# A two-block transformer kernel on one core: one opening stage, modulation parts in the key preparation, an unrolled first attention, and three weight buffers with indexed stores in the second experts

## What is computed

```python
# first block; x (1024, 1024), ctx (256, 1024)
mod_lat = silu(c) @ w_ada + b_ada            # w_ada (1024, 6144): six parts of 1024
mod_ctx = silu(c_ctx) @ w_ada + b_ada
sh1, sc1, gt1, sh2, sc2, gt2 = split(mod_lat, 6)
h_lat = rms_norm(x, norm_mix_g) * (1 + sc1) + sh1
h_ctx = rms_norm(ctx, norm_mix_g) * (1 + csc1) + csh1
proj = concat(h_ctx, h_lat) @ w_in
# differential attention, 4 heads, two score maps of width 64 per head, 1280 keys
a = softmax(s[0]) - lam * softmax(s[1]);  out = a @ v
# ... gated linear attention, out projection, then
x = x + gt1 * y;  h2 = rms_norm(x, norm_ffn_g) * (1 + sc2) + sh2
x = x + gt2 * moe(h2)                         # 32 experts, top 2
# second block: recurrent branch, causal attention, and at its end
h = h + moe_2(rmsnorm(h, norm2_g))            # 64 experts of hidden width 256, top 2
```

## Time and profile before

| | |
|---|---|
| median of 3 runs | 3930.11 us (3925.04 to 3935.51) |
| profiled execution | 3926.85 us, its span 3925.1 us |
| PE busy | 3098.5 us (79%) |
| DVE busy | 1792.8 us (46%) |
| ACT busy | 1248.2 us (32%) |
| POOL busy | 242.1 us (6%) |
| moved by DMA | 712.57 MB, mean 182 GB/s |

### The profile page before, as it was taken

How to read it: one execution, slowest core, us unless ns; L and a number is a source line. 1 busy time by engine, 2 the same in 40 slices (tenths; PEclk the granted TensorE clock), 3 DMA queues, 4 the chain that set the end, 5 groups by cost and what they waited for, 6 DMA issues and landing times. The chain is left out here.

```text
span 3925.1 us, 41291 instructions
## 1 busy us (share of the span) xinstructions
PE 3098.5 (79%) x14820; PEld 2213.1 (56%) x14820; DVE 1792.8 (46%) x2609; ACT 1248.2 (32%) x1544; POOL 242.1 (6%) x348
## 2 busy tenths in 40 slices
PE   6599966775657799999369789868999896777772
PEld 2488864453546688888257688744565783222220
DVE  0611126665655798888466411235655434111112
ACT  0301103444321577777345411223333310000001
POOL 0000021000000100000100000013000100000001
PEclk8699958997878799999679899989799996888886
DMA  6322117002043799999431132220001446999995
GB/s 284 114 74 91 60 48 284 0 0 72 28 158 123 297 408 406 405 406 401 175 95 38 31 96 81 82 74 10 1 1 38 155 149 237 417 421 422 421 422 237
DMA packets 192239, 712.57 MB, mean 182 GB/s; under 512 B 26564, under 2 KB 62071, under 8 KB 140664
## 3 DMA queue, kind: packets, MB, share of 16 engines
q1 hardware_dynamic: 144024, 575.25, 38.3%
q10 hardware_dynamic: 29664, 68.60, 4.5%
q0 software_dynamic: 18432, 67.12, 4.4%
HBM read 593.04 MB, written 117.87 MB: 181 GB/s over the span
## 5 line engine op out<-in xcount | busy, mean ns | idle before, releaser
L316 DVE TENSOR_TENSOR exp_w_low<-exp_raw,exp_w_high 128x2048 fp32r<-128x2048 f32 x192 | 437.1, 2290 | 70.7 <-ACT exp_w_high L2147 70.7
L2147 ACT CAST exp_w_high<-exp_raw 128x2048 fp32r<-128x2048 f32 x192 | 366.8, 1912 | 135.1 <-PE exp_ps_y L2119 58.3
L2355 PE MATMUL exp_ps_g<-exp_gu,exp_xT 128*64 128x512 f32 x1024 | 270.7, 689 | 125.2 <-DMA exp_gu<-in_exp_w 122.9
L2355 PEld LDWEIGHTS exp_ps_g<-exp_gu,exp_xT 128*64 128x64 f32 x1024 | 82.7, 158 | 292.8 <-issue 223.6
L2093 PE MATMUL exp_ps_g<-exp_w_low,exp_xT_high 128*128 128x512 f32 x512 | 206.5, 403 | 5.7 <-DVE exp_xT_low L316 5.7
L2094 PE MATMUL exp_ps_g<-exp_w_high,exp_xT_low 128*128 128x512 f32 x512 | 203.5, 397 | 0.0
L2095 PE MATMUL exp_ps_g<-exp_w_high,exp_xT_high 128*128 128x512 f32 x512 | 203.4, 397 | 0.0
L325 PE MATMUL inproj_ps<-inproj_w_high,h1T_high 128*128 128x512 f32 (+1 forms) x528 | 203.3, 385 | 0.0
L324 PE MATMUL inproj_ps<-inproj_w_high,h1T_low 128*128 128x512 f32 (+1 forms) x528 | 203.2, 385 | 0.0
L323 PE MATMUL inproj_ps<-inproj_w_low,h1T_high 128*128 128x512 f32 (+1 forms) x528 | 203.1, 385 | 0.0
L2464 DVE TENSOR_TENSOR exp_h<-exp_sg,exp_ps_g 128x256 f32<-128x256 f32 x32 | 19.5, 611 | 384.3 <-ACT exp_sg L2411 384.3
(11 more groups left out here) (546 smaller groups left out, 6853.1 us busy)
## 6 DMA issues: line engine op xcount, KB each, us to landing
exp_gu<-in_exp_w SPq DMA_DIRECT2D x64, 2048.0 KB, 17.6
exp_raw<-in_expert_w_gate SPq DMA_DIRECT2D x64, 1024.0 KB, 7.0
exp_raw<-in_expert_w_up SPq DMA_DIRECT2D x64, 1024.0 KB, 7.3
exp_raw<-in_expert_w_down SPq DMA_DIRECT2D x64, 1024.0 KB, 7.9
exp_dn<-in_exp_w SPq DMA_DIRECT2D x32, 2048.0 KB, 12.5
scratch_y<-exp_y ACTq DMA_DIRECT2D x64, 512.0 KB, 8.2
ada_slab<-in_w_ada SPq DMA_DIRECT2D x16, 1536.0 KB, 14.7
scratch_y<-da_zero SPq DMA_DIRECT2D x1, 15872.0 KB, 61.2
```

What stands on the lines that cost most here:

```text
L316: return nc.vector.tensor_tensor(low, x, high.bitcast(F32), ALU.subtract)
L2147: nc.scalar.copy(w_h[:, c], raw[:, b]).then_inc(w_high, 1)
L2355: last = nc.tensor.matmul(ps_g[side(e)], xT[:, par, k, side(e)], gu[:, par, :, e, k, :], start=(k == 0), stop=(k == KD - 1))
```

## The change

1. The constants, both tables, the first two modulation parts and the first normalisation become one block, `opening`. Only 2048 of the 6144 columns of `w_ada` are read there, in eight slabs that all have their own place, and all ten row tiles too. Four lanes are multiplied together. ACT squares the tiles, with the copies of the sums after the fifth. An `end_stage` follows.
2. Parts 2, 5, 3 and 4 are made in `diff_prepare`: 16 slabs of 1 MB in four buffers, a step of products behind each tile's turn, the bias as a product with a row of ones. The tiles of queries and keys get four buffers.
3. The first attention is written out over its 32 units without a loop. The turn of the weights runs two units behind the scores, the product with the values three; there are three buffers of weights. The queries are read where they are, without POOL's copy.
4. The second experts get a third pair of weight buffers. Slots without a token carry an index outside the tensors, and such rows are left out of the gather and of the store, which POOL now does by index. All of `y2` is filled with zeros in the first attention, not its overflow rows alone. `route` names the rows for both expert stages with four vector operations more.

```diff
+def opening(core, inp, tables, tiles, hT):
...
+                load_rows(0)
+                for k in range(KD):
+                    sp.dma_start(slab[:, k], w[:, k, 0:RUN]).then_inc(w_loaded[k], 16)
+                for i, (rows, _, _) in enumerate(tiles):
+                    sp.dma_start(xt[:, i], rows).then_inc(x_loaded[i], 16)
+                load_rows(1)
...
+                pe.wait_ge(made, 4)
+                turn_rows_of(0)
+                pe.wait_ge(c_ready, 2)
+                for k0 in range(0, KD, LANES):
+                    for k in range(k0, k0 + LANES):
+                        pe.wait_ge(w_loaded[k], 16)
+                    for b in range(BANKS):
+                        for k in range(k0, k0 + LANES):
+                            lane = slice(k % LANES * LANE, (k % LANES + 1) * LANE)
+                            last = nc.tensor.matmul(ps[lane, b], cs[:, k], slab[:, k, b * BANK:(b + 1) * BANK],
+                                                    start=(k0 == 0), stop=(k0 == KD - LANES))
+                last.then_inc(streamed, 1)
...
+                for i in range(n):
+                    pe.wait_ge(xn_ready, i + 1)
+                    if i >= 2:
+                        pe.wait_ge(half_a, i - 1)
+                        pe.wait_ge(half_v, i - 1)
+                    for k in range(KD):
+                        last = nc.tensor.transpose(ps[:, i % 2 * 2 + k // 4, k % 4 * P:(k % 4 + 1) * P],
+                                                   xt[:, i, k * P:(k + 1) * P], core.ident[:])
+                    last.then_inc(turned, 1)
+                turn_rows_of(1)
...
+                    square(i)
+                    if i >= 1:
+                        root(i - 1)
+                    if i == EARLY:
+                        act.wait_ge(streamed, 1)
+                        for b in range(0, BANKS, 2):
+                            nc.scalar.copy(sums[:, b * BANK:(b + 1) * BANK], ps[:, b]).then_inc(sums_copied[0], 1)
+                root(n - 1)
...
+                def low(i):
+                    dve.wait_ge(high_done, i + 1)
+                    low_part(nc, hT[1][:, :, i * P:(i + 1) * P], ht[:, i % 2], hT[0][:, :, i * P:(i + 1) * P]) \
+                        .then_inc(low_done, 1)
+
+                for i in range(n):
+                    dve.wait_ge(turned, i + 1)
+                    if i >= 2:
+                        dve.wait_ge(low_done, i - 1)
+                    for k in range(KD // 2, KD):
+                        last = evacuate(op, i, k)
+                    last.then_inc(half_v, 1)
+                    if i >= 1:
+                        low(i - 1)
+                low(n - 1)
...
-        norm_transpose(core, "norm1", tiles, hT)
+        opening(core, inp, tables, tiles, hT)
+        core.end_stage()
...
-        U = 2 * DA_H
+        U = TT * DA_H
         GROUPS = [range(c, min(c + 4, KT)) for c in range(0, KT, 4)]
         G = len(GROUPS)
-        COPIER = [1 if gi == 1 else 0 for gi in range(G)]
-        PER = [COPIER.count(0), COPIER.count(1)]
+        assert G == 3
+        TURN_LAG, WEIGH_LAG = 2, 3
...
+                    for n in range(U + WEIGH_LAG):
+                        if n < U:
+                            scores(n)
+                        turning, weighing = 0 <= n - TURN_LAG < U, 0 <= n - WEIGH_LAG < U
+                        if turning:
+                            turn_group(n - TURN_LAG, 0)
+                        if weighing:
+                            weigh_group(n - WEIGH_LAG, 0)
+                            weigh_group(n - WEIGH_LAG, 1)
+                        if turning:
+                            turn_group(n - TURN_LAG, 1)
+                        if weighing:
+                            weigh_group(n - WEIGH_LAG, 2)
+                        if turning:
+                            turn_group(n - TURN_LAG, 2)
...
+                    for n in range(U + TURN_LAG):
+                        turning = 0 <= n - TURN_LAG
+                        if turning:
+                            copy_turned(act, nc.scalar.copy, 0, n - TURN_LAG, 0)
+                        if n < U:
+                            t, h = n // DA_H, n % DA_H
+                            if n >= TURN_LAG + 1:
+                                act.wait_ge(a_turned, (n - TURN_LAG) * G)
+                            for m in range(2):
+                                act.wait_ge(nb_ready, 2 * n + m + 1)
+                                sums = l0[:, t % 2, h:h + 1] if m == 0 else st[:, n % 2, 5:6]
+                                nc.scalar.activation(p[:, n % (TURN_LAG + 1), m], ps[m][:, 0:NK], ACT.Exp,
+                                                     bias=st[:, n % 2, 2 + m:3 + m], scale=SCALE,
+                                                     accum_out=sums).then_inc(e_done, 1)
+                        if turning:
+                            copy_turned(act, nc.scalar.copy, 0, n - TURN_LAG, 2)
...
+                    for n in range(U + WEIGH_LAG):
+                        if n < U:
+                            for m in range(2):
+                                maximum(n, m)
+                        if 0 <= n - TURN_LAG < U:
+                            copy_turned(dve, V.tensor_copy, 1, n - TURN_LAG, 1)
+                        if n >= WEIGH_LAG and (n - WEIGH_LAG) % DA_H == DA_H - 1:
+                            read_results((n - WEIGH_LAG) // DA_H)
+                        if 0 <= n - 1 < U:
+                            difference(n - 1)
+                    dve.wait_ge(o_read, TT)
...
+    ORDER = (2, 5, 3, 4)
+    CHUNKS = len(ORDER)
+    PAIRS = KD // 2
+    STEPS = CHUNKS * PAIRS
+    WB = 4
...
+                for i in range(XB):
+                    load_x(i)
+                for j, m in enumerate(ORDER):
+                    sp.dma_start(bias[:, j], b_ada[:, m]).then_inc(bias_loaded, 16)
+                for i in range(WB):
+                    load_slabs(i)
+                for i in range(XB, STEPS):
+                    if i < KT:
+                        load_x(i)
+                    load_slabs(i)
+                sp.dma_start(gain[:], inp["norm_ffn_g"][0].partition_broadcast(P)).then_inc(gain_loaded, 16)
                 sp.dma_start(v[:], proj[:, 2 * W:3 * W].rearrange("(t p) n -> p t n", p=P)).then_inc(v_in, 16)
...
+                pe.wait_ge(bias_loaded, 16 * CHUNKS)
+                for i in range(STEPS):
+                    if i < KT:
+                        turn(i)
+                    conditions(i)
+                    j = i // PAIRS
+                    if j >= 1 and i % PAIRS < 2:
+                        wide_row(j - 1, i % PAIRS)
+                for h in range(2):
+                    wide_row(CHUNKS - 1, h)
...
-                ch.mark(V.tensor_copy(rt.row_tok[:], ps_t[:, 0:NB]))
+                ch.mark(V.tensor_scalar(absent[:], ps_t[:, 0:NB], 0.0, NOWHERE, ALU.is_equal, ALU.mult))
+                ch.link(V.tensor_scalar(tokf[:], ps_t[:, 0:NB], -1.0, 0.0, ALU.add, ALU.max))
+                ch.mark(V.tensor_copy(rt.row_tok[:], tokf[:]))
+                ch.mark(V.tensor_tensor(rt.row_from[:], tokf[:], absent[:], ALU.add))
+                ch.mark(V.tensor_tensor(rt.row_to[:], own_row[:], absent[:], ALU.add))
...
+    BUFS = 3
...
+            self.load_down(sp, b, b)
+
+    def clear_tokens(self, nc):
+        for b in range(2):
+            nc.gpsimd.memset(self.x[b][:], 0.0).then_inc(self.x_cleared, 1)
...
-                    sp.wait_ge(gu_done, n + 1)
-                    weights.load_gate_up(sp, n, par)
-                    sp.wait_ge(y_done, n + 1)
-                    weights.load_down(sp, n, par)
-
-                with sp.Fori(0, E // 2 - 1) as it:
-                    for par in range(2):
-                        load(it + 1, par)
+                def load(n, buf):
+                    sp.wait_ge(gu_done, n)
+                    weights.load_gate_up(sp, n, buf)
+                    sp.wait_ge(y_done, n)
+                    weights.load_down(sp, n, buf)
+
+                BUFS = weights.BUFS
+                rounds = E // BUFS - 1
+                with sp.Fori(0, rounds) as it:
+                    for b in range(BUFS):
+                        load(it * BUFS + (BUFS + b), b)
+                for n in range(BUFS * (rounds + 1), E):
+                    load(n, n % BUFS)
...
+                                            bounds_check=T - 1, oob_is_err=False) \
                         .then_inc(x_loaded[par], 16)
 
+                def scatter(half, par):
+                    n = half * 2 + par
+                    for z in range(2):
+                        pool.wait_ge(y_copied[z], n + 2)
+                    nc.gpsimd.tensor_copy(rows_to[par][:], rt.row_to[:, bass.ds(n, 1)]).then_inc(places_named, 1)
+                    pool.wait_ge(places_named, n + 1)
+
+                    pool.sem_inc(rows_seen, 1)
+                    pool.indirect_dma_start(out=y_rows, out_offset=bass.IndirectOffsetOnAxis(ap=rows_to[par][:, 0:1], axis=0),
```

(14 more changed lines are left out.)

892 lines of the change are left out of this document (390 added, 502 removed).

## The result

The changed kernel takes 3799.0 us (median of four runs, 3797.6 to 3803.4) against 3927.6 of the kernel before in the same comparison (3918.5 to 3935.5): a ratio of 0.9675, 95% interval 0.9652 to 0.9698. The sign and most of the gain are as forecast. The size is not: 3754 was predicted, and the time lies 2 us above the upper end of the range.

What follows compares the result with a forecast made beforehand. Bounds by stage: load waits in the opening, partly used DMA and low clock in preparation, latencies in attention, full DMA in second experts. -86 + 12 - 51 - 50 + 1 = -174 from 3926.85 gave 3753, stated as 3754; range 3728 to 3797.

Steps and rivals of the forecast that it cites:

- Opening, -86: Start to the projection's first load: one block issuing all loads at once, projection starting at about 76 instead of 162.5 us.
- Key preparation, +12: Stage before the first attention: added slabs and products end it near 618 instead of 606 us; bounds 0 and +25.
- it hides in the 5.4 us, or nearly: Key preparation: TensorE's added work per step fits within the 5.4 us per tile that VectorE and POOL set.
- after the tenth step: Key preparation: from there six steps, four wide pairs and two copy rounds lie uncovered, 18 us, or 31 at lower clock.
- First attention, -51: The 32 attention units: three of four drains go, units take about 7.35 us, 247 us against 298; bounds -25 and -55.
- the drain 7.6: End of the first attention: emptying the pipeline after the last unit was priced at 7.6 us.
- Second experts, -50: Second expert stage: third buffer and skipped rows cut 218 MB to 198, 518 us to 473; bounds -10 and -56.
- so half of the gathers and stores goes: Second experts: 2048 token places for 4096 slots, so gathers and stores fall from 30 to 15.5 MB.
- Rival 1: Second experts: an index out of bounds still costs its transfer, 16.8 MB or 40 us come back: 3794; chance 0.12.
- Rival 2: Attention keeps 8.2 us per unit and the preparation runs cold: -25 for -51, +25 for +12, total 3793; chance 0.10.
- Rivals 3 and 5: Opening and rest gain less in many small places, 3776; or third weight buffer fills too late, 3768; together chance 0.14.
- the bounds of two terms at once, not all four: Whole kernel: how the range 3728 to 3797 was set from the bounds of the four stage terms.

Runs made afterwards that it cites:

- e9_mirror_pairs: The changed kernel with the slots of both experts mirrored within their 64 rows in every second pair of the second experts: 3787.0 us, ratio 0.9645.
- e10_last_direct: The changed kernel with the outputs of the last two expert pairs stored by plain DMA of all 128 rows on ScalarE's queue: 3791.0 us, ratio 0.9648.
- e3_two_buffers: The changed kernel with two weight buffers in the second experts instead of three, unused rows still skipped: 3813.2 us, ratio 0.9712.
- e1_spread: The changed kernel with the second experts' rows in use spread over every eighth of the rows, not the front half: 3819.9 us, ratio 0.9729.
- e7_lags: The changed kernel with the first attention's transposes one unit behind instead of two, products two instead of three, some copies reordered: 3988.1 us, ratio 1.0159.

## Why the prediction was right or wrong, point by point

- **Opening, -86.** Right in size (-89.2), in part by luck. The forecast let ScalarE (done at 44) and VectorE (46.5) set the middle, with TensorE's column products over at 40. Measured, ScalarE's last root is done at 41.0, VectorE's last scaling at 42.7, and the column products end last, at 43.0: TensorE had the sums' products ready at 29.9, but ScalarE copies them only behind its fifth tile, from 33.63, and the column products then took 6.96 us for 5.26. Two errors of about 3 us met. From the first tile on it went as forecast, 28.4 us for 28.7.
- **Key preparation, +12.** The mechanism was right (TensorE's work uncovered behind the last turn), the size was not: +19.6, inside the bound of +25. The step that failed is "it hides in the 5.4 us, or nearly", with the count "after the tenth step". The tenth step and its wide row stand behind the last turn, 3.9 us, and the ninth's stand in front of it and held it up by 2.4. The price of a step of conditions, taken as 0.85 to 1.7 us from the merged records of the opening and summed at the lower end, is 1.91 alone, but 0.97 where two run interleaved; for the six it made 2.5 us more. The row of two wide products was right (2.4 taken, 2.1 to 2.2 measured). And it was not the lower clock: it was 0.97 to 1.00 there.
- **First attention, -51.** The unit came out as forecast (7.22 for 7.27), and 31 intervals took 231.9 us where the sum had 232.2. The term that was mis-sized is the drain, "the drain 7.6", 15.0 us with the last unit: it is 24.3. The forecast gives no rows for it; the kernel before, a less deep pipeline, takes 13.0 us from its last scores to its last output. The third unit to be emptied and the fall of the clock, 3.0 us, were left out.
- **Second experts, -50.** Volume, share of DMA and the third buffer's worth were right. The step that failed was "so half of the gathers and stores goes", as if it went from every engine alike. It went from the mean; the heaviest engine kept 356 rows of 512, not 256, and the last pairs wait for that engine. To the last weights it took 488.4 us where the sum had 473: 15 us, of which evening out the rows gave back 9.3, and 8.2 to the last store (e9_mirror_pairs, whose heaviest engine still has 286). The last weights to the last store took 2 us less than the 16 of the sum. Next, the close of the stage was costed at nothing: 5.6 us, POOL's drain, of which e10_last_direct gives back 5.4. Third, the start came 6.4 us later behind the routing, not 2.4: the gather's issue 1.7 later and its landing 8.3 us for the 4.5 of before, while the third pair's loads pass. Last, an error in the sum: from its own terms, 536.7 us between the first reload (3314.1) and the last store (3850.8) against 473 + 16, and 2.4 for the start, comes -45, and the text says -50. These make the 28.
- **Rival 1** (skipped rows are not free) had the right place for the wrong reason. A skipped row costs a packet of 4 bytes and 0.009 us; what is not free is the way in which the others lie. **Rival 2** had the preparation colder and the unit slower than they were; neither came. **Rivals 3 and 5** fell with the opening and e3_two_buffers.
- **The range** took in "the bounds of two terms at once, not all four". Three terms came out on the same side, each inside its own bound (-22 for -10, +20 for +25; the attention -42 for -25). Its upper end was too near for a sum of four.

## What to carry to other kernels

A saving of DMA bytes is worth what it takes from the most loaded of the 16 engines. With a full DMA stage, count rows by engine before you count megabytes, and look at how the DMA share falls at the end of the stage: here a slope meant unevenness. A step does not prove the opposite: with two buffers the rows lay as unevenly and the end was a step. Before trusting a rule read from one pattern, look for the packets in which the rival rule would differ; here three rows in 67 decided. At the end of a block ask which engine is released last and what it still has to do there. A deeper pipeline pays in its course and charges at its end; price the drain by its depth, and with the clock that rows of a similar pause show.

## What was not expected of the hardware

- An indirect store of 128 rows goes out as two halves of 64 rows on eight engines each, row p on engine (p div 4) mod 8 of its half; the times above fit the same for the gathers. Two kernels that move the same rows to other places differ by 21 us (e1_spread, 3819.9, and the changed kernel, 3799.0).
- A row whose index is out of bounds leaves a 4-byte packet of about 0.009 us; a row of 4096 bytes takes 0.160 us.
- With three buffers and uneven rows the engines run apart by some 18 us until the end (16 busy 18 us before the last packet, one at 2 us). With two buffers and the same rows 15 are busy until 2 us before the end, and the stretch runs at 401 GB/s, not 405; with two buffers and even rows, before the change, at 418.
- POOL's drain at the end of the block took 5.3 us behind an indirect store just landed and 10.5 us where the block's last indirect DMA lay further back (e10_last_direct); only the first delayed the other engines.
- Two steps of four 32-column products each that stand one behind the other in TensorE's order took 1.94 us together, one alone 1.91.
- In the drain the granted clock is 0.60 behind a wait of 1.48 us, and behind 5.26 us in every unit of e7_lags products again take 3.48 us for 1.95; a wait of 0.71 us in every unit of the steady course left it at 1.00.
